# First norm of a two-block transformer kernel: sums of squares on TensorE tile by tile, split values in PSUM, another order of the first loads, the root's table loaded early

## The reference, cut to what matters

```python
def rmsnorm(x, g):
    x32 = x.astype(jnp.float32)
    y = x32 * lax.rsqrt(jnp.mean(x32 * x32, axis=-1, keepdims=True) + EPS) * g.astype(jnp.float32)
    return y.astype(x.dtype)
...
h = rmsnorm(x, ln1[l])
z = jnp.einsum('btd,de->bte', h, w_in[l])
```

## Time and profile before

| | us |
|---|---|
| median of 3 executions | 2193.37 (2192.48 to 2194.1) |
| the profiled execution, whole time | 2191.03 |
| its span, first to last instruction | 2189.2 |
| TensorE busy | 2053.5 (94%) |
| VectorE busy | 1070.3 (49%) |
| ScalarE busy | 672.8 (31%) |
| GpSimd busy | 1040.6 (48%) |
| mean granted TensorE clock | 0.972 |

### The profile page before, as it was taken

How to read it: one execution, slowest core, us unless ns; L and a number is a source line. 1 busy time by engine, 2 the same in 40 slices (tenths; PEclk the granted TensorE clock), 3 DMA queues, 4 the chain that set the end, 5 groups by cost and what they waited for, 6 DMA issues and landing times.

```text
span 2189.2 us, 26361 instructions
## 1 busy us (share of the span) xinstructions
PE 2053.5 (94%) x9488; PEld 1655.3 (76%) x9488; DVE 1070.3 (49%) x1189; ACT 672.8 (31%) x1085; POOL 1040.6 (48%) x651
## 2 busy tenths in 40 slices
PE   5999989989999999999999997999899999989996
PEld 3777767877778878878878875887677778768775
DVE  6545554646531211212111258422777888763576
ACT  3345564132221001001000122112466666650312
POOL 1545555423733543543443364333456655653372
PEclk9999999988999999999999998999899999999997
DMA  3100000102211211211111122111000000011122
GB/s 138 50 20 21 20 10 29 49 30 106 96 39 48 72 53 48 67 57 48 54 61 48 48 79 76 39 50 39 30 20 19 19 29 19 19 39 48 39 77 96
DMA packets 31642, 106.65 MB, mean 49 GB/s; under 512 B 3449, under 2 KB 3641, under 8 KB 31577
## 3 DMA queue, kind: packets, MB, share of 16 engines
q1 hardware_dynamic: 27520, 96.14, 13.3%
q10 hardware_dynamic: 4066, 9.74, 1.2%
HBM read 101.51 MB, written 4.26 MB: 48 GB/s over the span
## 4 chain that ended last, share of the span: by engine, by line
PE 74%; DVE 11%; issue 6%; ACT 4%; POOL 3%; ACTq 0%; DVEq 0%; DMA 0%; POOLq 0%
PE ps L225 53%; PE ps L390 4%; PE ps L242 2%; PE ps L254 2%; POOL probs_lo L686 2%; PE ps L630 2%; PE ps L618 1%; PE ps L631 1%; DVE mx L731 1%; DVE h_lo L371 1%; PE ps L637 1%; PE ps L617 1%; PE ps L616 1%; DVE tmp L1777 1%; DVE x L1779 1%
## 5 line engine op out<-in xcount | busy, mean ns | idle before, releaser
L1949 POOL TENSOR_TENSOR w_hi<-w_raw,zero 128x1024 fp32r<-128x1024 f32 (+2 forms) x173 | 322.5, 1864 | 815.7 <-PE ps L225 579.5
L1951 POOL TENSOR_TENSOR w_lo<-w_raw,w_hi 128x1024 fp32r<-128x1024 f32 (+2 forms) x173 | 421.1, 2434 | 13.6
L225 PE MATMUL ps<-h_hi,w_lo 128*128 128x512 f32 x1328 | 333.3, 393 | 5.5 <-DVE x L517 5.1
L225 PE MATMUL ps<-h_hi,w_hi 128*128 128x512 f32 x1328 | 328.0, 389 | 0.0
L225 PE MATMUL ps<-h_lo,w_hi 128*128 128x512 f32 x1216 | 300.4, 389 | 0.0
L225 PEld LDWEIGHTS ps<-h_hi,w_lo 128*128 128x128 f32 x1328 | 248.4, 189 | 60.3 <-issue 9.7
L225 PEld LDWEIGHTS ps<-h_hi,w_hi 128*128 128x128 f32 x1328 | 249.2, 188 | 51.8
L686 POOL TENSOR_TENSOR probs_lo<-probs,mla_p_hi 128x512 fp32r<-128x512 f32 x192 | 191.3, 1016 | 171.2 <-ACT probs L679 169.3
L225 PEld LDWEIGHTS ps<-h_lo,w_hi 128*128 128x128 f32 x1216 | 228.2, 188 | 47.6
L1391 DVE TENSOR_TENSOR tmp<-ps,tmp 128x1024 f32<-128x1024 f32 x22 | 26.9, 1224 | 370.3 <-PE ps L225 363.6
L731 DVE TENSOR_REDUCE mx<-ps 128x1 f32<-128x128 f32 (+1 forms) x192 | 140.9, 755 | 79.0 <-PE ps L662 44.4
(11 more groups left out here) (342 smaller groups left out, 3709.2 us busy)
## 6 DMA issues: line engine op xcount, KB each, us to landing
w_raw<-in_wpack SPq DMA_DIRECT2D x173, 512.0 KB, 3.3
x<-in_xT ACTq DMA_DIRECT2D x16, 512.0 KB, 7.9
out<-result SPq DMA_DIRECT2D x8, 512.0 KB, 2.9
p_raw<-in_pT ACTq DMA_DIRECT2D x1, 1024.0 KB, 4.8
pos_i<-in_pos SPq DMA_DIRECT2D x1, 512.0 KB, 6.3
const_stage<-in_consts SPq DMA_DIRECT2D x1, 404.0 KB, 3.3
vec<-in_vecs SPq DMA_DIRECT2D x1, 284.0 KB, 4.7
mla_q_hi<-c_neg ACTq DMA_DIRECT2D x16, 4.0 KB
```

What stands on the lines that cost most here:

```text
L225: last = nc.tensor.matmul(dst[:, half, :], w[slot][:, kt, :], a[:, i, t], start=(n == 0), stop=(n == total - 1))
L1949: nc.gpsimd.tensor_tensor(w_hi[s][:, kts, :], raw[s][:, kts, :], no_change[:, kts, :], ALU.add).then_inc(w_hi_done, 1)
L1951: nc.gpsimd.tensor_tensor(w_lo[s][:, kts, :], raw[s][:, kts, :], w_hi[s][:, kts, :].bitcast(F32), ALU.subtract)\
```

## The change

Squares: each of the eight squares of a half has a buffer of its own (`first_sq`, 128 x 512 each), written by ScalarE with no wait on VectorE. VectorE no longer adds them. TensorE takes each square as weights in 128 x 128 blocks against a column of ones, and accumulates over the eight feature tiles in PSUM: 32 matmuls for a half in place of 4. For half 0 all four blocks follow each square as it comes. For half 1 three blocks of tile k-1 stand ahead of half 0's projections of tile k, and the last tile's three blocks and the eight fourth blocks behind half 0's projections. The sums lie in banks 5, 6, 7 and 4 (half 0) or 7 (half 1), so each root is two activations. VectorE writes the scaled tile into PSUM (banks 1 and 3 for half 0, 4 and 6 for half 1) instead of `tmp`, and ScalarE and VectorE read it there. SyncE, after x's first half, loads weight units 0 and 1, then x's second half, then positions. ScalarE issues four loads of x instead of eight, and then loads the table set with the root, ahead of the squares.

```diff
--- before.py
+++ after.py
@@ -206,7 +206,7 @@
 
 
         two = dict(ms=2, rt=2, rv=2, diag=2, bc=2)
-        N1 = Norm(2 * DT, **two)
+        N1 = Norm(2 * DT, ssq=0, **two)
 
         N2 = Norm(2 * DT, sq=N_HALVED, ssq=N_HALVED + 1, **two)
 
@@ -1849,66 +1849,99 @@
             nc.scalar.activation(ang[2][CR, :], ang[0][CR, :], ACT.Sin, scale=0.5).then_inc(rope_a, 1)
             nc.scalar.activation(ang[2][SR, :], ang[0][SR, :], ACT.Sin).then_inc(rope_a, 1)
 
-        second_sq = at("second_sq", R_M + 16384, [P, T])
-        first_sq = (sq, second_sq)
-
-
-        def first_total_dve(dve, half, k):
-            i = half * DT + k
+        first_sq = [at(f"first_sq{k}", R_M + 16384 + 2048 * k, [P, HALF]) for k in range(DT)]
+
+        def first_split(k, half):
+
+            return PS[:, ((1, 3), (4, 6))[half][k % 2], :]
+
+        def first_split_dve(dve, half, k):
             c = cols(half)
-            N1.wait(dve, "sq", i + 1)
-            part = first_sq[k % 2]
-            if k == 0:
-                nc.vector.tensor_copy(ssq[:, c], part[:, c]).then_inc(N1["ssq"], 1)
-            else:
-                N1.wait(dve, "ssq", i)
-                nc.vector.tensor_tensor(ssq[:, c], ssq[:, c], part[:, c], ALU.add).then_inc(N1["ssq"], 1)
+            if k < DT:
+                if k >= 2:
+                    N1.wait(dve, "lo", half * DT + k - 1)
+                nc.vector.scalar_tensor_tensor(first_split(k, half), x[:, k, c], vec[:, V_LN1 + k:V_LN1 + k + 1], PS[:, 4 + half, :],
+                                               ALU.mult, ALU.mult).then_inc(N1["h"], 1)
+            if k >= 1:
+                N1.wait(dve, "hi", half * DT + k)
+                nc.vector.tensor_tensor(h_lo[:, k - 1, c], first_split(k - 1, half), h_hi[:, k - 1, c].bitcast(F32), ALU.subtract)\
+                    .then_inc(N1["lo"], 1)
 
         def first_norm_dve(dve):
 
-            for k in range(DT):
-                first_total_dve(dve, 0, k)
             dve.wait_ge(vecs_in, 16)
             dve.wait_ge(setup_done, N_SETUP)
-            half_diag(dve, N1, 0)
-            N1.wait(dve, "bc", 1)
-            for k in range(DT + 1):
-                half_split_dve(dve, N1, 0, k, gain_of(V_LN1))
-                if k < DT:
-                    first_total_dve(dve, 1, k)
-            half_diag(dve, N1, 1)
-            N1.wait(dve, "bc", 2)
-            for k in range(DT + 1):
-                half_split_dve(dve, N1, 1, k, gain_of(V_LN1))
+            for half in range(2):
+                half_diag(dve, N1, half)
+                N1.wait(dve, "bc", half + 1)
+                for k in range(DT + 1):
+                    first_split_dve(dve, half, k)
 
         def first_norm_act(act):
             def square(half, k):
-                i = half * DT + k
                 act.wait_ge(x_in[half * 4 + k // 2], 16)
-                if k >= 2:
-                    N1.wait(act, "ssq", i - 1)
-                nc.scalar.activation(first_sq[k % 2][:, cols(half)], x[:, k, cols(half)], ACT.Square).then_inc(N1["sq"], 1)
+                nc.scalar.activation(first_sq[k][:, :], x[:, k, cols(half)], ACT.Square).then_inc(N1["sq"], 1)
+
+            def hi(half, k):
+                N1.wait(act, "h", half * DT + k + 1)
+                nc.scalar.activation(h_hi[:, k, cols(half)], first_split(k, half), ACT.Copy).then_inc(N1["hi"], 1)
             for k in range(DT):
                 square(0, k)
             act.wait_ge(setup_done, N_SETUP)
-            half_root(act, N1, 0)
+            first_root(act, 0)
             for k in range(DT):
                 square(1, k)
-                half_split_act(act, N1, 0, k)
-            half_root(act, N1, 1)
+                hi(0, k)
+            first_root(act, 1)
             for k in range(DT):
-                half_split_act(act, N1, 1, k)
+                hi(1, k)
+
+
+
+        SUM_BANK = ((5, 6, 7, 4), (5, 6, 7, 7))
+
+        def first_block_pe(half, k, b):
+            col = half + (half == 1 and b == 3)
+            return nc.tensor.matmul(PS[:, SUM_BANK[half][b], col:col + 1], first_sq[k][:, b * P:(b + 1) * P], ones[:, 0:1],
+                                    start=(k == 0), stop=(k == DT - 1))
+
+        def first_sum_pe(pe, half, k):
+            N1.wait(pe, "sq", half * DT + k + 1)
+            for b in range(3):
+                first_block_pe(half, k, b)
+            if half == 0:
+                last = first_block_pe(half, k, 3)
+            elif k == DT - 1:
+                for i in range(DT):
+                    last = first_block_pe(half, i, 3)
+            if k == DT - 1:
+                last.then_inc(N1["ms"], 1)
+
+        def first_root(act, half):
+            N1.wait(act, "ms", half + 1)
+            three, c = PS[:, 5:8, half], half * 4
+            nc.scalar.activation(rt[:, c:c + 3], three, ACT.Sqrt, bias=eps, scale=1.0 / D)
+            fourth = PS[:, SUM_BANK[half][3], 2 * half:2 * half + 1]
+            nc.scalar.activation(rt[:, c + 3:c + 4], fourth, ACT.Sqrt, bias=eps, scale=1.0 / D).then_inc(N1["rt"], 1)
 
         def first_norm_pe(pe):
-            half_sum_pe(pe, N1, DT, 0)
+            for k in range(DT):
+                first_sum_pe(pe, 0, k)
             half_spread_pe(pe, N1, 0)
 
             def arrived(half, k):
-                if (half, k) == (1, 0):
-                    half_sum_pe(pe, N1, 2 * DT, 1)
+                if half == 0:
+                    if k:
+                        first_sum_pe(pe, 1, k - 1)
+                elif k == 0:
+                    first_sum_pe(pe, 1, DT - 1)
                     half_spread_pe(pe, N1, 1)
                 N1.wait(pe, "lo", half * DT + k + 1)
             project_by_half(pe, ((U_SMALL, pjA), (U_FV[0], FV_BANKS[0])), h_hi, h_lo, arrived, (True, False))
+
+        def x_load(eng, i):
+            c, k = cols(i // 4), i % 4 * 2
+            eng.dma_start(x[:, k:k + 2, c], xT[k * P:(k + 2) * P, c].rearrange("(k p) t -> p k t", p=P)).then_inc(x_in[i], 16)
 
         block = ctx.enter_context(nc.Block())
 
@@ -1917,13 +1950,17 @@
             sp.dma_start(stage[:, :], consts).then_inc(consts_in, 16)
             sp.dma_start(vec[:, :], vecs).then_inc(vecs_in, 16)
             sp.wait_ge(x_in[3], 16)
-            sp.dma_start(pos_i[:, :], pos).then_inc(pos_in, 16)
 
             def load(u, s):
                 sp.wait_ge(w_split, u + 1)
                 sp.dma_start(raw[s][:, :, :].rearrange("p k n -> p (k n)"), wpack[u, :, :] if isinstance(u, int) else
                              wpack[bass.ds(u, 1), :, :].rearrange("o p n -> (o p) n")).then_inc(w_loaded[s], 16)
-            with sp.Fori(0, N_UNITS // 2) as it:
+            for s in range(2):
+                load(s, s)
+            for i in range(DT // 2, DT):
+                x_load(sp, i)
+            sp.dma_start(pos_i[:, :], pos).then_inc(pos_in, 16)
+            with sp.Fori(1, N_UNITS // 2) as it:
                 for s in range(2):
                     load(it * 2 + s, s)
             if N_UNITS % 2:
@@ -1997,10 +2034,9 @@
             act.sem_inc(mla.pv_hi, 2)
             act.sem_inc(mla.p_lo_done, 2)
             act.sem_inc(gate_read, 1)
-            for i in range(DT):
-                c = cols(i // 4)
-                k = i % 4 * 2
-                act.dma_start(x[:, k:k + 2, c], xT[k * P:(k + 2) * P, c].rearrange("(k p) t -> p k t", p=P)).then_inc(x_in[i], 16)
+            for i in range(DT // 2):
+                x_load(act, i)
+            act.preload_act_table_set("sqrt_and_others")
             first_norm_act(act)
             small_act(act)
             fox_values_act(act, 0)
```

## The result

The changed kernel took 2197.1 us (median of 11 executions, 2195.92 to 2206.38) against 2192.86 for the kernel before in the same comparison: ratio 1.0037, 95% interval 1.0027 to 1.0048. It is slower, by 4.2 us at the median. But the eleven times are not one heap: six lie between 2195.9 and 2197.1, five between 2205.4 and 2206.4, with nothing between. The profiled execution is one of the long ones, 2205.46 us (span 2203.7), 14.4 us over the profiled one of before.

What follows compares the result with a forecast made beforehand. TensorE was taken to bound the kernel: 19.1 us later at half 1's sum, 0.2 for the root, 0.9 for the spread, +20.2 on 2191.03 gives 2211.2; with 2.3 to the median, 2213.5, range 2198 to 2217.

Steps and rivals of the forecast that it cites:

- the price of the sums: TensorE, one half's 64 sum records: 13.8 us at the low clock level, 7.6 us at the high one.
- The front: Half 0 up to its first projection: sums end at 21.2 us, scaling starts at 25.6, first projection at 27.8.
- The mix: Half 0's projections with half 1's sums between them: 3.86 us of TensorE a tile at the low clock level.
- scaling into PSUM: Half 1's scaled tiles written to PSUM: taken as zero extra, bound by 0 and 1 us for eight tiles.
- Between the two I choose the low level, by rows 8: TensorE's clock stays low throughout half 0, since 1.95 us of sums spoiled a dense stream in the profile; chance 0.6.
- rival B: The clock rises during half 0; if after two tiles, +6.3 us, 2199.7; chance 0.23.
- B's earliest rise: Clock rising after two tiles of half 0, at 34.2 us: +6.3 us; the range began just under it, at 2198.
- What I added for the second spread: Half 1's spread runs at the low clock level, 2.07 us instead of 1.13: 0.9 us more.
- C: The sums themselves raise the clock at about 13 us, ahead of half 0's projections: 2191.9; C and E together 0.10.
- D: The sums' weight loads hide beneath 512-column matmuls and between arriving squares: faster, 2187; chance 0.07.
- They take a wait at 28.1 away, but nothing would use them earlier: Early weights, units 0 and 1 both split by 23.7 us, remove a wait but bring no earlier use.
- my bound for that meeting, 0.9 us: Half 0's diagonal beside GpSimd's remainder of unit 1: nothing to 0.9 us of delay, 0.5 taken.

Runs made afterwards that it cites:

- experiment 2: Changed kernel with all of half 1's sums behind half 0's projections instead of between them; 2200.17 us, ratio 1.0038 to the kernel before.
- experiment 1: The changed kernel timed once more with no edit; median 2199.2 us, ratio 1.0045 to the kernel before.
- x_first: Changed kernel with the loads in the order of before, early weights undone; 2199.72 to 2210.16 us, ratio 1.0058 to the kernel before.
- experiment 3: Changed kernel with 12 projections and 12 sum records in turn, instead of 6 and 6; 2195.16 to 2197.44 us, ratio 1.0016.
- experiment 4: Changed kernel with each sum matmul streaming 128 columns of ones instead of one; 2192.93 to 2195.68 us, ratio 1.0012.
- Experiment 5: Runs on what held the diagonal, among them `x_first` and `moves_only`; changed kernel with VectorE's sums 2188.68 us, with ScalarE's diagonal too 2183.39 us.
- moves_only: Kernel before with only the new order of loads and the early table load; 2191.23 us, ratio 0.9990.

## Why the prediction was wrong

The direction was right, and so were the price of the sums and the place of the delay. The course of the clock was not, and with it the size. I gave 2213.5 and 2198 to 2217; the median is 2197.1.

**The front** held. Sum records of 0.216: 0.215. End of the sums 21.2: 21.3. First scaling 25.6: 26.05. First projection 27.8: 28.22, where 0.3 of the missing 0.4 is the diagonal, put at 0.5 over its old length and measured 0.8 over it.

**The mix** held for as long as the clock was low: 3.86 us a tile forecast, 2.77 + 1.07 = 3.84 measured. Half 1 kept its pace (60.91 to 63.07 for the first projection, 2.2 us as forecast), and scaling into PSUM cost nothing (1.41 us for two, as in the earlier trace rows).

**The step that failed** is "Between the two I choose the low level, by rows 8". From a clock that fell behind 1.95 us of sums I concluded that the mix would hold it low for all eight tiles. By their times no execution did. The long ones came nearest: in the profiled one the clock was low for six tiles and into the sums ahead of the seventh, 15.2 us at half 1's scaling instead of 20.2. Six of the eleven executions were rival B, priced at 2199.7 and measured at 2195.9 to 2197.1. What rows 8 show is true of a stretch of sums only, as experiment 2 repeated. In the mix the clock rose after all: 7, 11 or 23 us behind the first projection in the three profiles of it (experiment 1, `x_first`, the changed kernel), and in pieces twice as long in experiment 3 at about 33.8, with all eleven times in the short group. The two groups were not forecast at all, and where the median falls between them is luck: six short executions of eleven put it under my range, and the same kernel in experiment 1 had 2199.2, inside it. The lower edge should have had room below B's earliest rise. B's own price was 1 us too low at half 1's scaling (52.0 by its steps, 52.98 measured) and 2.7 us too high at the end, of which 2.3 was the difference that I added between the profiled execution and the median. What I added for the second spread held in the long execution: it ran at the low level there, 2.07 us (58.80 to 60.87).

**Rivals C and D.** C did not occur: 64 records without a gap stayed at 0.215 us. The sentence of the Trainium skill that C takes at its word ("TensorE: Matmul & The Clock Gate", "What's actually happening") does not hold for these sums, and the measurement decides. Experiment 4 made the front's part of C occur, with 128 columns in place of one behind the same weight loads. D falls: a group of six records in the mix adds 1.28 us to a tile (3.84 less six projections of 0.427), 0.21 each, nothing hidden.

**"They take a wait at 28.1 away, but nothing would use them earlier"** was wrong as well, without showing in the sum. Experiment 5 puts the early weights at 3.3 us of the first projection, since they get GpSimd out of the diagonal's way. And my bound for that meeting, 0.9 us over the diagonal's own length, was far too low in general: it was 4.1 us with late weights (4.96 less 0.87) and 5.1 in experiment 4. I had bounded it by the diagonal's length, where the other side's instructions set it; rows 4 had warned of this, with an addition of 2.84 us instead of 0.69. With a faster front the early weights are themselves the trouble (6.00 us in experiment 4).

**What stays open.** The shift at half 1's scaling does not come through unchanged. The time less that moment goes from 2141.9 to 2147.6 us over the profiled executions. The moves alone (`moves_only`) gained 2.07 us at half 1's scaling and nothing in the profiled time (2191.26 against 2191.03). Part of this is the clock again, in a later stage. The chains, first of the kernel before, then of `moves_only`:

```profile
116.67 6.58 PE ps L225 x24
124.25 5.52 PE ps L225 x24
```

```profile
114.97 7.42 PE ps L225 x24
123.41 5.52 PE ps L225 x24
```

A lead of 1.70 us has become 0.84. The granted clock was 0.50 from about 112 to 119 in the kernel before, and from about 108.7 to 119 in `moves_only`, so the kernel that arrived earlier ran longer at the low level. Where the rest goes was not followed up. Nor was it settled why the rise in the mix of single tiles comes at about 35, 43 or 51: between the two executions of the changed kernel nothing differs in the program.

## What to carry over

Count what a matmul streams, not only how long it is busy: here a sum with one moving column paid a full weight load (0.215 us at the low level), and a long row of them cost the work behind it its clock (experiment 2). Turning it round, with ones as the weights and the data moving, gave the two fastest plans with the sums on TensorE, at the price of squares rounded to fp32r. When a change moves work on GpSimd, look at which VectorE operations with all operands in SBUF fall beside it; giving such a short operation on the critical path to ScalarE paid here. And where a clock that can stand at two levels bounds the stage, forecast two times, not one.

## What the hardware showed that I had not expected

The clock falls while TensorE is busy with not a gap: 2.3 us into 64 one-column sums (experiment 2). 128 moving columns per weight load cost next to no time over one (0.11 us a record at the high level, either way), and with them the clock rose within the 64 records and stayed up through the mix of experiment 4 once it had risen there. Four VectorE blocks of 128 columns, 0.87 us when alone, took 4.96 to 6.00 us beside GpSimd's splitting, while a scaling from SBUF and PSUM beside it took its usual 0.75. A VectorE reciprocal costs 6.6 ns a column, 3.38 us for 512; with four columns it took 0.18 us and was never visible.
